# Expert rows of a two-layer encoder step in 52 blocks of 32 rows, by column groups of TensorE, with five expert buffers

## The chip, the cores and the metric

The kernel runs on one core of a Trainium2 chip. The metric is the device time of one execution in microseconds (us), the median of several. Engines are named as in the profile: PE is TensorE's matmuls, PEld its weight loads, DVE VectorE, ACT ScalarE, POOL GpSimd, SP SyncE. A name with a q (SPq, DVEq) is an engine's sequencer.

## The reference, cut to what matters

Two layers of an encoder run over 592 token rows of width 1024 in f32. Each has a mixer and then a mixture of experts. The change is in the experts (and in the layer norm after them):

```
scores = sigmoid(x @ router_w)                       # 16 experts in 4 groups of 4
grouped = scores + router_bias; best group; top 2 experts inside it
for e in range(16):
    h = silu(x @ w_gate[e]) * (x @ w_up[e])          # 1024 -> 256
    y = y + (h @ w_down[e]) * combine[..., e]        # 256 -> 1024
x = layer_norm(ALPHA * x + y)
```

Each token goes to two experts, so there are 1184 pairs of token and expert per layer, 74 per expert on average.

## The kernel before, in words

The program is written out by hand for each engine; every order is that of the code, and engines wait for each other by semaphores. The experts of a layer (`experts(l)` on each engine) work as follows.

**Slots.** Each of the 16 experts has 128 slots. VectorE ranks the tokens of each expert and writes, for each expert, five one-hot tiles of 128x128 (line 2155); TensorE multiplies them with the token numbers (line 1314), which gives the token of every slot. POOL gathers the rows of 128 slots with an indirect DMA (line 960) into one of two buffers. Where an expert has more tokens than slots, the rest goes into overflow blocks. Each engine has a loop over at most `NOV` = 9 of them (lines 768, 966, 1413, 1738, 2216), whose iterations do nothing past the count that was found.

**Work of one expert.** TensorE transposes the 128 gathered rows (line 1359, 8 transposes), ACT and DVE copy them out, then 8 matmuls of a 128x128 stationary slice of rows with 128x512 moving weights (gate and up side by side) make the hidden values in one PSUM bank (line 1371). ACT takes the exponential (line 1727), DVE forms silu and the product (lines 2182 to 2185), TensorE transposes the result (line 1379), DVE copies it, and 4 matmuls (line 1390) multiply it with the down weights, halves of 512 columns. ACT and DVE copy one half each (lines 1734, 2208), and SP stores the 128 rows to `y_rows` (line 760). Each f32 matmul call is two instructions in the trace. TensorE's order in step e is: gate and up of e, transposes of e-1's hidden values, transposes of e+1's rows, down of e-1.

**Weights.** An expert's weights are 1 MB gate, 1 MB up, 1 MB down (lines 723 to 725), all on SP's queue, in four buffers: experts e with e % 4 below 2 in `ring`, the others in `wexp` in the arena. SP loads experts 2 and 3 when attention ends, 0 and 1 when the output projection ends (`ring` holds that projection's weights until then), and expert e+4 when the down product of e is done.

**After the experts.** SP's queue also loads the next layer's weights, four items after the store of expert 13 (line 718). When the last stores have landed, POOL gathers two rows per token from `y_rows` (line 942); in layer 0 DVE adds them and norms (lines 2303 to 2330), after its loop over overflow blocks; in layer 1 TensorE adds them by diagonal matmuls (lines 1326 to 1328). The residual rows and the norm's parameters are loaded by POOL between the gathers of experts 2 and 3.

**Elsewhere.** The router's partial sums (line 1123) are matmuls with 32 stationary columns whose outputs go to PSUM partitions 0, 32, 64 and 96 in turn, so that four of them lie in four column groups of the array:

```
for k in range(KD):
    c = 32 * (k % 4)
    last = pe.matmul(ps[c:c + 32, 512 * half:512 * half + n], w[:, k, :],
                     xT[:, k, lo + n * half:lo + n * half + n], start=(k < 4), stop=(k >= 4))
```

Early in layer 0, POOL issues nine stores of zeros to the overflow rows (line 836).

## Time and profile before

| | us |
|---|---|
| median of 3 runs | 1348.32 (1345.34 to 1348.69) |
| the profiled execution's own time | 1348.82 |
| its span | 1347.0 |
| TensorE matmuls busy | 1208.0 (90%) |
| VectorE busy | 600.8 (45%) |
| ScalarE busy | 266.9 (20%) |
| lines 1371 and 1390 (gate and up, down) | 229.5 and 115.8 busy |

The span runs from the first to the last recorded instruction; the execution's own time is 1.8 us more. A line's busy time is the sum over its instructions with overlaps counted once.

### The profile page before, as it was taken

Reading aid. Unit: us, or ns where it says so; the run is one execution under the profiler, and the core shown is the slowest. Engines: PE = TensorE matmul, PEld = TensorE weight load, DVE = VectorE, ACT = ScalarE, POOL = GpSimd, SP = SyncE. Lnnn points to the kernel's source line nnn. Section 1 sums busy time; section 2 is a strip of 40 time slices with the busy share of each in tenths; the row PEclk is TensorE's granted clock in tenths of the full one; section 3 lists DMA queues with packets and bytes.
Section 4 is the critical chain, followed back from the end, with each engine's and each line's share of the span. In section 5 each row is a group of like instructions: output and inputs, shape, how many; then the busy total and the mean of one; then the engine's idle time right before and its main releaser. Section 6 shows DMA issues by size and latency. Waiting matters only on the chain.

```text
span 1347.0 us, 13706 instructions
## 1 busy us (share of the span) xinstructions
PE 1208.0 (90%) x4719; PEld 689.0 (51%) x4719; DVE 600.8 (45%) x1412; ACT 266.9 (20%) x630; POOL 223.6 (17%) x390
## 2 busy tenths in 40 slices
PE   8999999998899489999749899999999939999966
PEld 4447777544644244444325455775764424444422
DVE  2178888503624537433355120530533345744316
ACT  1204434212300001111102223322320001111110
POOL 0105444222002120000063200000001111000013
PEclk9999999999999789999969999999999959999978
DMA  8113012353461669999652410000125168999733
GB/s 335 62 63 141 1 63 79 126 187 25 60 218 57 213 195 363 362 361 369 239 188 76 167 63 0 1 0 1 63 64 187 55 230 283 356 362 370 262 141 121
DMA packets 109156, 219.23 MB, mean 163 GB/s; under 512 B 5145, under 2 KB 72281, under 8 KB 107937
## 3 DMA queue, kind: packets, MB, share of 16 engines
q1 hardware_dynamic: 90544, 153.35, 32.3%
q0 software_dynamic: 18256, 64.20, 15.2%
q8 instruction: 39, 0.64, 0.2%
q10 hardware_dynamic: 288, 0.80, 0.2%
q14 instruction: 29, 0.23, 0.1%
HBM read 183.44 MB, written 34.86 MB: 162 GB/s over the span
## 4 chain that ended last, share of the span: by engine, by line
PE 82%; DVE 8%; issue 4%; DMA 2%; ACT 2%; POOL 1%; DVEq 0%; POOLq 0%; ACTq 0%; SPq 0%
PE pair L1371 16%; PE pair L1280 10%; PE pair L1029 10%; PE pair L1390 8%; PE pair L1040 5%; PE pair L1146 5%; PE pair L1212 5%; PE pair L1464 3%; PE pair L1249 3%; PE pair L1516 2%; PE pair L1359 2%; PE pair L1070 2%; PE pair L1247 1%; PE pair L1496 1%; PE pair L1230 1%
## 5 line engine op out<-in xcount | busy, mean ns | idle before, releaser
L1029 PE MATMUL pair<-ring,xT 128*128 128x512 f32 (+1 forms) x320 | 138.9, 593 | 0.0
L1371 PE MATMUL pair<-ring,arena 128*128 128x512 f32 x256 | 117.0, 611 | 3.5 <-DVE arena L2173 3.5
L1371 PE MATMUL pair<-arena 128*128 128x512 f32 x256 | 112.5, 592 | 0.0
L1029 PEld LDWEIGHTS pair<-ring,xT 128*128 128x128 f32 (+1 forms) x320 | 57.7, 182 | 75.6 <-issue 75.1
L1146 PE MATMUL pair<-xT,ring 128*128 128x296 f32 x320 | 85.1, 421 | 6.1 <-ACT arena L1552 3.0
L807 POOL TENSOR_SCALAR small<-small 128x1 f32<-128x1 f32 (+3 forms) x45 | 15.7, 349 | 419.8 <-DVE small L2054 376.6
L1371 PEld LDWEIGHTS pair<-ring,arena 128*128 128x128 f32 x256 | 49.9, 196 | 66.6 <-issue 66.6
L2193 DVE COPY arena<-pair 128x256 f32<-128x256 f32 x32 | 13.6, 424 | 156.3 <-PE pair L1379 156.3
L829 POOL TENSOR_TENSOR arena<-arena 128x128 f32<-128x128 f32 x140 | 56.6, 438 | 158.0 <-PE pair L1072 87.9
L1371 PEld LDWEIGHTS pair<-arena 128*128 128x128 f32 x256 | 48.6, 190 | 61.2 <-issue 61.2
L1212 PE MATMUL pair<-arena 128*128 128x264 f32 (+5 forms) x280 | 76.6, 403 | 2.6 <-issue 1.4
L960 POOL DMA_INDIRECT arena<-x_rows,ints x32 | 31.0, 970 | 287.5 <-PE pair L1359 236.6
L1986 DVE TENSOR_REDUCE small<-pair 128x1 f32<-128x144 f32 (+4 forms) x40 | 22.4, 560 | 120.3 <-PE pair L1217 120.2
L1146 PEld LDWEIGHTS pair<-xT,ring 128*128 128x128 f32 x320 | 60.4, 193 | 25.6 <-issue 9.0
L1280 PE MATMUL pair<-ring,mixT 128*128 128x512 f32 (+1 forms) x160 | 72.1, 593 | 1.0 <-issue 1.0
L1280 PE MATMUL pair<-ring,xT 128*128 128x512 f32 (+1 forms) x160 | 71.9, 592 | 0.0
L1390 PE MATMUL pair<-arena 128*128 128x512 f32 x128 | 58.2, 597 | 5.2 <-DVE arena L2193 5.2
L1040 PE MATMUL pair<-arena,ring 128*128 128x296 f32 (+1 forms) x224 | 62.1, 438 | 0.0
L1464 PE MATMUL pair<-ring,xT 128*128 128x512 f32 (+3 forms) x160 | 58.8, 523 | 1.1 <-ACT xT L1543 1.1
L1390 PE MATMUL pair<-ring,arena 128*128 128x512 f32 x128 | 57.6, 592 | 0.0
L2183 DVE RECIPROCAL arena<-arena 128x256 f32<-128x256 f32 x32 | 56.1, 1753 | 1.1
L2046 DVE SCALAR_TENSOR_TENSOR rb<-xr,pair 128x1024 f32<-128x1024 f32 (+1 forms) x10 | 12.2, 1221 | 95.7 <-PE pair L1280 95.7
(347 smaller groups left out, 1859.3 us busy)
## 6 DMA issues: line engine op xcount, KB each, us to landing
arena<-in_moe_w_gate SPq DMA_DIRECT2D x16, 1024.0 KB, 6.8
arena<-in_moe_w_up SPq DMA_DIRECT2D x16, 1024.0 KB, 9.4
arena<-in_moe_w_down SPq DMA_DIRECT2D x16, 1024.0 KB, 11.3
ring<-in_moe_w_gate SPq DMA_DIRECT2D x16, 1024.0 KB, 7.3
ring<-in_moe_w_up SPq DMA_DIRECT2D x16, 1024.0 KB, 9.9
ring<-in_moe_w_down SPq DMA_DIRECT2D x16, 1024.0 KB, 11.6
y_rows<-arena SPq DMA_DIRECT2D x32, 512.0 KB, 9.7
ring<-in_even_w_in SPq DMA_DIRECT2D x5, 2048.0 KB, 7.3
```

What stands on the lines that cost most here:

```text
L829: last = pool.tensor_tensor(dst, both, mid, ALU.subtract)
L960: pool.indirect_dma_start(xg[:, e % 2, :], None, x_rows[2 * l], bass.IndirectOffsetOnAxis(ap=sloti[:, e:e + 1], axis=0)).then_inc(xg_in[e ...
L1029: last = pe.matmul(ps[0:P, 0:n], xT[:, k, 128 * i:128 * i + P], w[:, k, :], start=(k == 0), stop=(k == chunks - 1))
L1040: last = pe.matmul(ps[0:w.shape[2], 512 * s:512 * s + n], w[:, k, :], src[:, k, n * s:n * s + n], start=(k == 0), stop=(k == chunks - 1))
L1146: last = pe.matmul(ps[0:w.shape[2], 512 * s:512 * s + n], w[:, k, :], xT[:, k, n * s:n * s + n], start=(k == 0), stop=(k == KD - 1))
L1212: last = pe.matmul(ps[0:P, lo:lo + cols], q_, k_, start=(c == 0), stop=(mask is None and c == len(lq) - 1))
L1249: last = pe.matmul(out, vb[j], pT[:, n % 2, 128 * j:128 * j + P], start=False, stop=(j == nb - 1))
L1280: last = pe.matmul(ps[0:P, 512 * half:512 * half + 512], mixed(k, i), w[:, k, :], start=(k == 0), stop=(k == KD - 1))
L1371: last = pe.matmul(bank, xgT[:, e % 2, k, :], gu[:, k, :], start=(k == 0), stop=(k == KD - 1))
L1390: last = pe.matmul(psum[2][:, 512 * half:512 * half + 512], hT[:, e % 2, 128 * k:128 * k + 128], dn[:, k, 512 * half:512 * half + 512], st ...
L1464: last = pe.matmul(ps[0:P, lo:lo + n], xT[:, k, 128 * i:128 * i + P], w[:, k, :], start=(k == 0), stop=(k == KD - 1))
L2183: chain(dve.reciprocal(eg[:, b, :], eg[:, b, :]))
```

## The change

**Slots.** Experts have 96, 96, 128 and 96 slots in turn (`CAPS`), 1664 in all: 52 blocks of 32 in 13 tiles of 128 (`NX`). A tile's four blocks belong to one expert or to two neighbouring ones: tile 0 is three blocks of expert 0 and one of expert 1, tile 1 two of expert 1 and two of expert 2, and so on (`BLOCKS`); tile 8 is all expert 10, and the last, tile 12, one block of expert 14 and three of 15. All per-expert steps (gather, transposes, copies, store) are now per tile. `NOV` is 12.

**Matmuls.** In gate and up and in down, each matmul is replaced by four, one for each block: 32 stationary columns, the weights of the block's expert as the moving operand, the block's 32 PSUM partitions as output.

**Weights.** Gate and up lie side by side in DRAM, and both tensors are stored there as they lie in SBUF, so that a partition's 4096 (gate and up) or 2048 (down) words are one contiguous run. There are five buffers: two in `wexp`, two in `ring`, the fifth in `xT` (gate and up) and `mixT` (down). Experts 0 and 1 are loaded at attention's end, 2, 3 and the down weights of 4 after the output projection, the rest of 4 after the router's partial sums. For experts 5 to 15, SP issues gate and up when gate and up of the last tile of the buffer's earlier expert are in PSUM; ACT issues the down weights on its own queue, after its wait for that tile's down product and ahead of its copy of it.

**Around.** The residual rows and the norm's parameters are loaded after the last gather; tile 4's residual goes into a buffer that comes free later, and is loaded after tile 0's combine. The four items of the next layer's weights are issued after the stores of tile 10 (the first) and tile 11 (the other three). The slot numbers take two more small VectorE steps. The one-hot tiles are one instruction per expert in a tile, and the first group is tile 0 alone, then two tiles each.

```diff
-NOV = 9
-NSLOTS = (NE + NOV) * 128
+CAPS = [96, 96, 128, 96] * 4
+BASE = [sum(CAPS[:e]) for e in range(NE)]
+NX = sum(CAPS) // 128
+NOV = 12
+NSLOTS = (NX + NOV) * 128
+BLOCKS = [[next(e for e in range(NE) if BASE[e] <= 128 * x + 32 * j < BASE[e] + CAPS[e]) for j in range(4)]
+          for x in range(NX)]
+LAST = [max(x for x in range(NX) if e in BLOCKS[x]) for e in range(NE)]
+NB = 5
+PLACE = [e % NB for e in range(NE - 1)] + [1]
+BEFORE = [max((p for p in range(e) if PLACE[p] == PLACE[e]), default=None) for e in range(NE)]
...
+    parts["base"] = np.broadcast_to(np.array(BASE, np.float32), (128, 16))
+    parts["caps"] = np.broadcast_to(np.array(CAPS, np.float32), (128, 16))
 
     s3 = s[:, :, None]
...
+        x_far = [arena[:, lo:lo + D] for lo in (0, 3552)]
+        assert 3552 + D <= yg_at
         qng = r4.take(QL + KVL)
 
         def residual(s, i):
 
-            return x_far[i - 2] if s % 2 == 1 and i >= 2 else xr[:, i % 2, :]
+            return x_far[i - 2] if s % 2 == 1 and i in (2, 3) else xr[:, i % 2, :]
 
 
...
+        IX_GROUPS = [range(max(x, 0), x + 2) for x in range(-1, NX, 2)]
         LAST_IX = len(IX_GROUPS) - 1
...
-            gu = base[:, 0:2 * SLOT].rearrange("p (k n) -> p k n", k=KD)
-            dn = base[:, 2 * SLOT:3 * SLOT].rearrange("p (k n) -> p k n", k=2)
-            return gu, dn
-
-        gate_d = a["moe_w_gate"].rearrange("l e (k p) n -> (l e) p k n", p=128)
-        up_d = a["moe_w_up"].rearrange("l e (k p) n -> (l e) p k n", p=128)
-        down_d = a["moe_w_down"].rearrange("l e (k p) n -> (l e) p k n", p=128)
+            b = PLACE[e]
+            if b < 4:
+                base = (wexp if b < 2 else ring)[:, (b % 2) * 3 * SLOT:(b % 2) * 3 * SLOT + 3 * SLOT]
+                gu, dn = base[:, 0:2 * SLOT], base[:, 2 * SLOT:3 * SLOT]
+            else:
+                gu = xT[:, :, :].rearrange("p k t -> p (k t)")[:, 0:2 * SLOT]
+                dn = mixT[:, :, :].rearrange("p k t -> p (k t)")[:, 0:SLOT]
+            return gu.rearrange("p (k n) -> p k n", k=KD), dn.rearrange("p (k n) -> p k n", k=2)
+
+        gu_d, down_d = a["moe_w_gate_up"], a["moe_w_down"]
 
         def mixed(k, i):
 
...
+            def load_gate_up(l, e):
+                sp.dma_start(expert_place(e)[0], gu_d[l * NE + e]).then_inc(we_in[PLACE[e]].sem, 16)
+
+            def load_down(l, e):
+                sp.dma_start(expert_place(e)[1], down_d[l * NE + e]).then_inc(we_in[PLACE[e]].sem, 16)
+
             def load_expert(l, e):
-                gu, dn = expert_place(e)
-                s = we_in[e % 4].sem
-                sp.dma_start(gu[:, :, 0:DE], gate_d[l * NE + e]).then_inc(s, 16)
-                sp.dma_start(gu[:, :, DE:2 * DE], up_d[l * NE + e]).then_inc(s, 16)
-                sp.dma_start(dn, down_d[l * NE + e]).then_inc(s, 16)
+                load_gate_up(l, e)
...
+                sp.wait_ge(*pe_full[("wo", l, 4)])
                 load_expert(l, 2)
                 load_expert(l, 3)
-                sp.wait_ge(*pe_full[("wo", l, 4)])
-                load_expert(l, 0)
-                load_expert(l, 1)
-                for e in range(NE):
-                    if e + 4 < NE:
-                        sp.wait_ge(*dn_ps[(l, e)])
-                        load_expert(l, e + 4)
-                    sp.wait_ge(*y_sa[(l, e)])
-                    sp.wait_ge(*y_sd[(l, e)])
-                    sp.dma_start(y_rows[l][128 * e:128 * e + 128, :], yb[:, e % 2, :]).then_inc(y_st[e % 2].sem, 16)
-                    if l == 0 and e == 13:
-                        for n in range(n_items0, n_items0 + 4):
-                            load_item(n)
+                load_down(l, 4)
+                sp.wait_ge(*pe_full[("lp", l, 1)])
+                load_gate_up(l, 4)
+                for x in range(NX + 1):
+                    if x < NX:
+                        sp.wait_ge(*gu_ps[(l, x)])
+                        for e in FREED[x]:
+                            load_gate_up(l, e)
+                    if x >= 1:
+                        d = x - 1
+                        sp.wait_ge(*dn_ps[(l, d)])
+                        sp.wait_ge(*y_sa[(l, d)])
+                        sp.wait_ge(*y_sd[(l, d)])
+                        sp.dma_start(y_rows[l][128 * d:128 * d + 128, :], yb[:, d % 2, :]).then_inc(y_st[d % 2].sem, 16)
+                        if l == 0 and d == LAST[12]:
+                            load_item(n_items0)
+                        if l == 0 and d == LAST[13]:
+                            for n in range(n_items0 + 1, n_items0 + 4):
+                                load_item(n)
 
                 mk = ov[l]
                 sp.wait_ge(*ix_sb[(l, LAST_IX)])
                 count = sp.value_load(ovi[0:1, 0:1], min_val=0, max_val=NOV)
                 with sp.Fori(0, NOV) as b:
                     with sp.If(count > b):
...
+                if s % 2 == 1 and i == 4:
+                    pool.wait_ge(*(pe_full[("cb", 1, 0)] if s == 3 else cb_sb[(0, "first")]))
+                elif s % 2 == 1 and i >= 2:
+                    pool.wait_ge(*dn_ps[(s // 2, LAST[10])])
                 elif i >= 2:
                     pool.wait_ge(*r_mv[(s, i - 2)])
...
 
             def gather_rows(l, i):
...
-                        load_ln_params(2 * l + 1)
-                        for i in range(NT):
-                            load_residual(2 * l + 1, i)
                     pool.indirect_dma_start(
                         xg[:, e % 2, :], None, x_rows[2 * l],
                         bass.IndirectOffsetOnAxis(ap=sloti[:, e:e + 1], axis=0)).then_inc(xg_in[e % 2].sem, 16)
+                load_ln_params(2 * l + 1)
+                for i in range(4):
+                    load_residual(2 * l + 1, i)
                 m = ov[l]
-                pool.wait_ge(*xgT_ps[(l, NE - 1)])
+                pool.wait_ge(*xgT_ps[(l, NX - 1)])
                 count = pool.value_load(ovi[0:1, 0:1], min_val=0, max_val=NOV)
                 with pool.Fori(0, NOV) as b:
                     with pool.If(count > b):
...
             pool.dma_start(qng[:, 0:QL], a["mla_q_norm_g"][0].partition_broadcast(128)).then_inc(mg_in.sem, 16)
             pool.dma_start(qng[:, QL:QL + KVL], a["mla_kv_norm_g"][0].partition_broadcast(128)).then_inc(mg_in.sem, 16)
             layer_norm_row(1, 0)
+            load_residual(1, 4)
             scale_row(1, 1)
             for i in range(NT):
                 if i + 1 < NT:
...
             def gate_up(l, e):
-                pe.wait_ge(*we_in[e % 4][(l, e)])
+                for x in sorted(set(BLOCKS[e])):
+                    pe.wait_ge(*we_in[PLACE[x]][(l, x)])
                 pe.wait_ge(*xgT_sa[(l, e)])
                 pe.wait_ge(*xgT_sd[(l, e)])
                 if e >= 2:
                     pe.wait_ge(*h_sb[(l, e - 2)])
-                gu, _ = expert_place(e)
                 bank = psum[1][:, 512 * (e % 2):512 * (e % 2) + 512]
                 for k in range(KD):
-                    last = pe.matmul(bank, xgT[:, e % 2, k, :], gu[:, k, :], start=(k == 0), stop=(k == KD - 1))
+                    for j, x in enumerate(BLOCKS[e]):
+                        c = slice(32 * j, 32 * j + 32)
+                        last = pe.matmul(bank[c, :], xgT[:, e % 2, k, c], expert_place(x)[0][:, k, :],
+                                         start=(k == 0), stop=(k == KD - 1))
                 last.then_inc(gu_ps.sem, 1)
 
             def hidden_t(l, e):
...
-                        last = pe.matmul(psum[2][:, 512 * half:512 * half + 512], hT[:, e % 2, 128 * k:128 * k + 128],
-                                         dn[:, k, 512 * half:512 * half + 512], start=(k == 0), stop=(k == 1))
+                        for j, x in enumerate(BLOCKS[e]):
+                            c = 32 * j
+                            last = pe.matmul(psum[2][c:c + 32, 512 * half:512 * half + 512],
+                                             hT[:, e % 2, 128 * k + c:128 * k + c + 32],
+                                             expert_place(x)[1][:, k, 512 * half:512 * half + 512],
+                                             start=(k == 0), stop=(k == 1))
                 last.then_inc(dn_ps.sem, 1)
 
             def experts(l):
                 rows_t(l, 0)
-                for e in range(NE + 1):
-                    if e < NE:
...
                     if e >= 1:
                         act.wait_ge(*dn_ps[(l, e - 1)])
+                        for n in FREED[e - 1]:
+                            act.dma_start(expert_place(n)[1], down_d[l * NE + n]).then_inc(we_in[PLACE[n]].sem, 16)
...
                     chain(ts(wts, wts, 1.0 / ALPHA, None, ALU.mult))
-                chain(ts(ovn, cnt, 128.0, None, ALU.is_gt))
-                for m in (256.0, 384.0, 512.0):
+                chain(tt(cnt, cnt, const("caps"), ALU.subtract))
+                chain(ts(ovn, cnt, 0.0, None, ALU.is_gt))
+                for m in (128.0, 256.0, 384.0):
...
 
-                for e in IX_GROUPS[g]:
-                    for i in range(NT):
-                        last = ts(oneh[:, e % 2, i, :], iotab[:, :], 1.0, rk1[:, i, e:e + 1], ALU.add, ALU.is_equal)
+                for x in IX_GROUPS[g]:
+                    for e in sorted(set(BLOCKS[x])):
+                        lo, n = 32 * BLOCKS[x].index(e), 32 * BLOCKS[x].count(e)
+                        r = 128 * x + lo - BASE[e]
+                        last = tt(oneh[:, x % 2, :, lo:lo + n], iotab[:, r:r + n].unsqueeze(1).to_broadcast([128, NT, n]),
+                                  rk1[:, :, e:e + 1].to_broadcast([128, NT, n]), ALU.is_equal)
                     last.then_inc(oh_sb.sem, 1)
 
...
               "cache_fox_logf": np.asarray(inputs["cache_fox_logf"])[0, 0].T}
+    tiles_of = lambda w: np.asarray(w).reshape(2 * NE, -1, 128, w.shape[3]).transpose(0, 2, 1, 3)
+    inputs = {**inputs, "moe_w_down": tiles_of(inputs["moe_w_down"]),
+              "moe_w_gate_up": tiles_of(np.concatenate([inputs["moe_w_gate"], inputs["moe_w_up"]], 3))}
```

Three places at which the order of instructions changes follow. On TensorE, in layer 0's experts, one step in full, before (line 1390 is down, 1371 gate and up, 1379 and 1359 the transposes):

```order
L1314 MATMUL pair<-cstb,arena 128x2 x10
L1379 MATMUL pair<-cst,arena 128x128 x2
L1359 MATMUL pair<-cst,arena 128x128 x8
L1390 MATMUL pair<-ring,arena 128x512 x4
L1371 MATMUL pair<-arena 128x512 x8
```

and with the change (1409 and 1386 are the transposes, 1421 is down, 1400 gate and up):

```order
L1341 MATMUL pair<-cstb,arena 128x2 x10
L1409 MATMUL pair<-cst,arena 128x128 x2
L1386 MATMUL pair<-cst,arena 128x128 x8
L1421 MATMUL pair<-arena 32x512 x16
L1400 MATMUL pair<-ring,arena 32x512 x32
```

The transposes are the same; 4 matmuls of 128 stationary columns became 16 of 32, and 8 became 32.

On ScalarE, from one exponential to the next (and the copies after it), before (1718 copies transposed rows, 1734 the down product, 1727 is the exponential):

```order
L1727 ACTIVATE arena<-pair 128x256
L1718 COPY arena<-pair 128x512
L1734 COPY arena<-pair 128x512
L1727 ACTIVATE arena<-pair 128x256
L1718 COPY arena<-pair 128x512
L1734 COPY arena<-pair 128x512
```

and with the change, at the step that frees two experts' buffers (1751, 1769 and 1760 are the same three):

```order
L1760 ACTIVATE arena<-pair 128x256
L1751 COPY arena<-pair 128x512
L1766 DMA ring<-in_moe_w_down 128x2048
L1766 DMA mixT<-in_moe_w_down 128x2048
L1769 COPY arena<-pair 128x512
L1760 ACTIVATE arena<-pair 128x256
```

Two loads of down weights stand ahead of the copy of the down product.

On SyncE, at the end of layer 0's experts, before (718 are the next layer's weights, 760 the stores of expert rows, 767 the read of the overflow count):

```order
L723 DMA arena<-in_moe_w_gate 128x8x256
L724 DMA arena<-in_moe_w_up 128x8x256
L725 DMA arena<-in_moe_w_down 128x2x1024
L760 DMA y_rows<-arena 128x1024 x3
L718 DMA ring<-in_mla_w_in 128x8x512
L718 DMA ring<-in_mla_w_in 128x8x320
L718 DMA ring<-in_mla_w_uk 128x2x1024
L718 DMA ring<-in_mla_w_uv 128x2x1024
L760 DMA y_rows<-arena 128x1024 x2
```

and with the change (731, 783 and 792 are the same):

```order
L783 DMA y_rows<-arena 128x1024 x2
L734 DMA arena<-in_moe_w_gate_up 128x4096
L783 DMA y_rows<-arena 128x1024 x3
L731 DMA ring<-in_mla_w_in 128x8x512
L783 DMA y_rows<-arena 128x1024
L731 DMA ring<-in_mla_w_in 128x8x320
L731 DMA ring<-in_mla_w_uk 128x2x1024
L731 DMA ring<-in_mla_w_uv 128x2x1024
L783 DMA y_rows<-arena 128x1024
```

Three of the four items now stand between the last two stores, where before all four stood ahead of the last two.

## Rows read from the trace of the kernel before

**Rows 1.** Page, part 2: TensorE's busy tenths and clock in 40 slices.
```profile
PE   8999999998899489999749899999999939999966
...
PEclk9999999999999789999969999999999959999978
```

**Rows 2.** Windows: us, busy by engine, clock, DMA share, GB/s; start, then expert stage.
```profile
5.00:15.00 10.00, 9.45 (x28) 6.89 (x29) 0.00 (x0) 0.00 (x0) 0.00 (x0) 1.00 1.04 432
600.00:640.00 40.00, 40.00 (x125) 19.95 (x124) 17.16 (x27) 5.64 (x11) 2.87 (x3) 1.00 1.05 371
```

**Rows 3.** Timeline of TensorE late in layer 0's experts: start, duration, line.
```profile
639.95 7.03 PE L1371 MATMUL pair<-arena 128*128 128x512 f32 x16
...
647.90 3.60 PE L1390 MATMUL pair<-ring,arena 128*128 128x512 f32 x8
651.34 7.03 PE L1371 MATMUL pair<-arena 128*128 128x512 f32 x16
```

**Rows 4.** Timelines of the column-grouped line 1123, and its weight loads (ns min/median/max).
```profile
1076.59 1.92 PE L1123 MATMUL pair<-xT,vecs 128*32 128x512 f32 x16 [1.10 <-ACT xT L1543]
...
235.47 2.20 PE L1123 MATMUL pair<-xT,vecs 128*32 128x296 f32 x32
...
L1123 PEld LDWEIGHTS pair<-xT,vecs x96: 106/110/177, 235.5 to 1082.6; 128*32 128x32 f32 x96
```

**Rows 5.** Chain of waits: start, duration, what; last steps ahead of layer 0's experts.
```profile
466.72 1.73 DVE arena L2155 x10
...
469.45 0.83 issue
470.28 4.26 DMA arena<-x_rows,ints
...
477.49 9.22 PE pair L1371 x16
```

**Rows 6.** Timeline of VectorE: one product over 128x256.
```profile
490.39 0.42 DVE L2184 TENSOR_TENSOR arena<-pair,arena 128x256 f32<-128x256 f32 x1
```

**Rows 7.** Line 725: time on SyncE's queue (ns min/median/max), then landing.
```profile
L725 SPq DMA_DIRECT2D ring<-in_moe_w_down x16: 1531/2718/4786, 447.8 to 1234.8; - x16
...
DMA to landing us min/median/max: 9.8/11.4/14.3
```

**Rows 8.** Timeline of ScalarE: copy of an expert's output, next exponential.
```profile
500.42 0.59 ACT L1734 COPY arena<-pair 128x512 f32<-128x512 f32 x1 [2.85 <-PE pair L1390]
507.28 0.39 ACT L1727 ACTIVATE arena<-pair 128x256 f32<-128x256 f32 x1 [6.28 <-PE pair L1371]
```

**Rows 9.** Timeline of SyncE's queue at the end of layer 0's experts.
```profile
652.81 1.44 SPq L718 DMA_DIRECT2D ring<-in_mla_w_in  x2
...
663.61 5.17 SPq L760 DMA_DIRECT2D y_rows<-arena  x2
```

**Rows 10.** Chain of waits from layer 0's last store to its combine.
```profile
668.42 5.31 DMA y_rows<-arena
...
675.98 0.06 DVEq L2217
...
676.69 0.06 DVEq L2217
...
681.30 1.29 DVE arena L2303
```

**Rows 11.** Layer 1: chain, loop on TensorE (ns, first and last start), timeline.
```profile
1296.25 2.73 DMA y_rows<-arena
...
L1413 PEldq COMPARE_BRANCH  x18: 86/220/229, 669.9 to 1303.7; - x18
...
1306.64 2.04 PE L1326 MATMUL pair<-xr,arena 128*128 128x512 f32 x2 [11.20 <-DMA arena<-y_rows,ints]
```

**Rows 12.** Timeline of POOL: the nine stores of zeros and the work after them.
```profile
118.19 4.99 POOL L836 DMA_DIRECT2D y_rows<-xr  x9
124.10 2.59 POOL L829 TENSOR_TENSOR arena<-arena 128x128 f32<-128x128 f32 x7 [0.92 <-ACT arena L1567]
```

110 lines of the change are left out of this document (54 added, 56 removed).

## The prediction

> **What bounds the kernel now.** I read the page first, for the engine that is busy: TensorE's matmuls are busy nine tenths or more in most slices of the span, and the granted clock is nearly full in most of them [rows 1]. Then windows of the expert stage: in 40 us of it TensorE is busy all 40 at full clock, and the DMA engines have no gap either, moving 371 GB/s [rows 2]. Two resources are full at once, so the timeline has to say who waits. In it gate and up of one expert starts at 639.95 and that of the next at 651.34, 11.39 us later, with nothing idle between: 7.03 for gate and up, 3.60 for down (their tails overlap what follows), the transposes in the rest [rows 3]. So TensorE sets the pace and DMA only just keeps up. What is worth something here is a whole step of 11.39 us, as long as the weights come in time.
>
> **Term 1, three steps fewer per layer.** 16 steps become 13. A step keeps its transposes, copies, exponential and store; what must be priced is the new matmul form, since a step now issues 96 instructions on 32 columns (64 for gate and up, 32 for down) where it issued 24 on 128. The kernel has this form already: line 1123 puts four matmuls of 32 stationary columns and different moving data into four column groups. Its 16 instructions over 512 moving columns take 1.92 us, its 32 over 296 take 2.20 [rows 4]. At full width, 16 instructions over 512 take 7.03 [rows 3]. 8 take 3.60 [rows 3], so an instruction is (7.03 - 3.60) / 8 = 0.43 and the tail of the last one 0.17; without that tail the grouped form takes 1.75 / 4 = 0.44 per four. Four groups run in the time of one, with their weight loads inside. So 64 instructions are 16 such fours, 6.9 us as before, and the step stays at 11.39. Six steps go: 6 x 11.39 = **-68.3 us**. Nothing else covers this time, since TensorE is idle nowhere in the step.
>
> **Term 2, the head.** The first gather now waits for the one-hots of tile 0 alone. Before, the chain has ten instructions, 1.73 us, then 0.83 until POOL starts, 4.26 for the rows [rows 5]. Now there are two, over 480 and 160 elements per partition; a product over 256 takes 0.42 [rows 6], so at most 1.05. Gain 0.7 a layer: **-1.4**. Against it: expert 4's gate and up are the last of 9.4 MB (experts 2 and 3, the rest of 4) queued from 447 on. At 432 GB/s, which loads of long runs reach early in the kernel [rows 2], they end at 469; at 371 at 472.5, and then the gather shares the engines for up to 3 us. I count nothing and keep 3 us for the range, since the new layout has the long runs.
>
> **Term 3, the loop over overflow blocks.** `NOV` goes from 9 to 12, on five engines. On DVE in layer 0 the loop starts when the last store lands and ends just as the gathered rows come, at 681.30; one empty iteration is 676.69 - 675.98 = 0.71 us [rows 10]. Three more are **+2.1** in full. In layer 1 TensorE's loop ends at 1303.9, and the combine starts at 1306.64, released by the gather [rows 11]; 2.1 more ends it at 1306.0, just hidden. ACT's and POOL's loops end earlier still.
>
> **Term 4, the last store of layer 0.** It is queued behind loads on SP's queue. Now, with four items issued from 652.81 on, ahead of the last two stores [rows 9], it takes 5.31 to land [rows 10], in layer 1 without them 2.73 [rows 11]. With the change three of them, 3.4 MB, stand between the last two stores. From the first of these stores to the landing of the last is 10.2 us now (4.8 between the two issues, of which the second lasts some 0.4 of the 5.17 [rows 9], then 5.31). Then 3.4 MB and two stores of 0.52 MB must pass: 4.5 MB at 432 to 371 GB/s is 10.4 to 12.1, and the landing about 1.4 behind the last byte, so 11.8 to 13.5. I take the middle: **+2.5**.
>
> **What I cost at nothing.** ACT's loads: one of 1 MB is on SP's queue for 1.5 to 4.8 us there [rows 7], behind two others; on ACT it stands ahead of the copy of the down product, and ACT has 6.28 us free behind that copy [rows 8]. One fits. Where two stand together (tiles 3 and 7) the worst is 9.6 us, and the copy would be up to 2.2 too late for the next down product (11.39 - 3.43 = 8.0 us after the last): 9 us in all for four places, kept below. Queued behind the ACT load are that copy, the next exponential, and with it DVE's silu, which has a whole gate and up of slack. Residual rows and norm parameters come some 20 us ahead of the combine; tile 4's residual is issued by POOL after tile 0's store and has three tiles of work ahead of it. Two more VectorE steps on slot numbers lie in a step in which VectorE is mostly idle. POOL's three further stores of zeros are about 1.7 us; its next work waited 0.92 for ACT anyway [rows 12], so at most 0.8 shows.
>
> **The weights' supply.** Expert 15 is needed when tile 12 starts, 12 x 11.39 = 137 us after tile 0. From the end of tile 0's gate and up (7 us), 11 x 3.15 MB of weights, 23 transfers of 0.52 MB, and up to 5.2 MB of residuals, parameters and the first item must pass: 46.7 to 51.9 MB. At 432 GB/s that ends at 115 to 127, at 371 at 133 to 147. The new layout makes 371 the bound that holds least. Ends: no stall, or 10 us a layer. I take no stall, since 432 is what loads of such runs reached.
>
> **Sum.** -68.3 - 1.4 + 2.1 + 2.5 = -65.1. The span 1347.0 becomes 1281.9, the execution 1283.7 (it is 1.8 longer). The profiled execution, 1348.8, lies 0.5 above the median of the runs, so **1283** for the median, with 1276 to 1291 for this case by the bounds above.
>
> **Rivals.** (B) *Late weights.* Loads of down weights are issued when the product is done, and for experts 6, 7, 8, 12, 13 and 15 the tile that needs them starts 11.4 us later. Line 725's land 9.8 to 14.3 after issue, median 11.4 [rows 7]. For it: these are just too long. Against: there 2 MB stand ahead on the same queue, here none. At 14.3, 2.9 late at twelve places is 35 us; with the 9 of ACT the worst is 1327; half of the lateness, 22, gives 1305.
> (F) *Supply stays at 371 GB/s* and all of the 51.9 MB stand ahead: 10 us late per layer, 1303. For it: only the first microseconds show more. Against: there the runs were long, as they are now. The Trainium skill (DMA: Bandwidth & Descriptors, Specifications) gives about 358 GB/s as a core's limit at the HBM; by an estimate from it the last weights come up to 15 us late per layer, and the sum is 1313. The 432 of this trace [rows 2] does not agree with that as a limit for this core alone.
> (C) *The four groups overlap less.* If in each four one weight load of 0.11 us [rows 4] does not hide, a four takes 0.54; 24 fours a step, 26 steps, +0.11 each: +69, so 1352. Against it: the 0.44 of line 1123, weight loads included. The Trainium skill (TensorE: Matmul & The Clock Gate, Measured speedup vs the span model) says three column tiles of 32 over 512 gained 2.38 times, not 3; by an estimate from that a four takes 0.54 too.
> (D) *Slower.* The weight loads and streams of the groups go one after the other, as they may when the moving data come from four places of SBUF. With all four loads outside, 0.44 more per four, 24 x 26 x 0.44 = 275: 1558. It decides from 0.53 per four on (65 us over 624 fours is 0.10). Line 1123 speaks against this too, its moving data also lie in four places.
> (E) *It does not do what it says:* an expert has more tokens than slots, and an overflow block runs. Counting the router's choices on the reference's inputs, I get at most 92 for an expert of 96 slots and 97 for one of 128. One block would be in series: rows 4.3, weights 11.4, matmuls 10, hidden values and stores 7, about 33 us: 1316.
>
> **Chances.** Forecast 0.76; B 0.11; F 0.04; C 0.04; D 0.03; E 0.02. The range 1276 to 1304 takes in the forecast with its bounds, F, and the lower half of B. A difference under 0.3% (4 us) cannot be told from none. Faster: forecast, B, F, E, 0.93. C straddles the line: 0.03 same, 0.01 slower, and with D slower is 0.04.
>
> **What would show it.** Right: gate and up starts 11.4 us apart in 13 steps, 7.0 us for its 64 instructions; TensorE idle nowhere in them; the first gather 0.7 earlier; DVE's loop 2.1 longer and on the chain; the last store of layer 0 landing near 7.8 us after issue. Wrong: a wait of TensorE on the loads of `in_moe_w_down` or `in_moe_w_gate_up`, most of all in tiles 4 to 6, 9, 10 and 12, with a clock of 0.5 behind it (B, F); steps over 13 us with no idle time (C, D); line 1454 or the gathers of overflow blocks in the trace (E).

## The result and the profile after

The changed kernel takes **1308.04 us** (median of 4, 1306.13 to 1308.65), the kernel before beside it 1348.51: a ratio of 0.9701, 95% interval 0.9682 to 0.9720. That is 40 us faster, where 65 were forecast, and above the range of 1276 to 1304. The profiled execution took 1306.13, with a span of 1303.9 us.

The page, part 2, TensorE and its clock beside [rows 1]: still a full engine, with much the same dips.
```profile
PE   8999999999899759999549899999999957999965
...
PEclk9999999999999969999869999999999978999978
```

Cut at five places, the span of 1347.0 became 1303.9 like this (the forecast by its own terms in the last column):

| stretch | before | after | change | forecast |
|---|---|---|---|---|
| start to first gate/up, layer 0 | 477.5 | 475.3 | -2.2 | -0.7 |
| layer 0: to the end of the last down | 190.1 | 163.8 | -26.3 | -34.2 |
| to the first gate/up of layer 1 | 437.9 | 444.7 | +6.8 | +3.9 |
| layer 1: to the end of the last down | 189.9 | 165.7 | -24.2 | -34.2 |
| to the end | 51.6 | 54.4 | +2.8 | 0 |

Only the expert stages gain, and each 8 to 10 us less than three steps of 11.39. The chain of waits says why. First an undisturbed step, late in layer 0:
```profile
599.56 6.87 PE pair L1400 x64
606.43 0.37 PE pair L1409 x2
...
607.67 3.57 PE pair L1421 x32
611.24 0.84 PE pair L1400 x5
```
(1400 is gate and up, 1409 and 1386 the transposes, 1421 down.) Nothing is idle, and gate/up of one tile starts 11.68 us before the next (611.24 - 599.56), not 11.39. The timeline of the same step, which can be set beside [rows 3], has 8.22 from the start of gate/up to the start of down (599.38 to 607.60), where [rows 3] has 7.95, and 3.46 from down to the next gate/up, against 3.44. So the work itself costs what [rows 4] promised, and 0.27 us lie between gate/up and down, where full-width transposes stand between column-grouped matmuls.

At the head of layer 0 the one-hots are shorter, but the gather behind them is longer than the 4.26 of [rows 5]:
```profile
463.82 0.91 DVE arena L2194 x2
...
466.61 5.72 DMA arena<-x_rows,ints
```
In the 5.7 us of the gather, SyncE's queue still moves 0.95 MB of weights; in the 4.3 us before it moved none.

The second piece, the chain at tile 3 of layer 0:
```profile
499.30 0.18 DVE ints L2206
499.48 0.26 issue
499.74 9.02 DMA arena<-x_rows,ints
508.80 1.09 PE pair L1386 x8
```
Its rows are asked for when VectorE has written their slot tokens, at 499.5, land 9.0 us later, and TensorE has waited 2.4 us. In layer 1 it is 2.5.

The third, tile 9, the chain in layer 0 and in layer 1:
```profile
582.28 3.57 PE pair L1421 x32
585.86 1.82 issue
587.68 7.07 PE pair L1400 x64
...
1193.85 2.56 issue
1196.42 8.77 PE pair L1400 x64
```
This "issue" ends when the weights of expert 12 are there, the last block of tile 9. ScalarE issued its down weights at 574.24, and they took 13.3 us. The row of `in_moe_w_down` between 573 and 583 us says so; the second fence has the two transfers of gate and up, for experts 13 and 14, that SyncE's queue had issued before them:
```profile
L1766 ACTq DMA_DIRECT2D ring<-in_moe_w_down x1: 334/334/334, 574.2 to 574.2; - x1
...
DMA to landing us min/median/max: 13.3/13.3/13.3
```
```profile
569.42 0.33 SPq L734 DMA_DIRECT2D ring<-in_moe_w_gate_up  x1
569.79 0.55 SPq L734 DMA_DIRECT2D xT<-in_moe_w_gate_up  x1
```
These down weights are not what tile 9's gate and up work on. One semaphore counts both loads of an expert, and `gate_up` waits for its full count (line 1391). Expert 12's gate and up weights were issued at 557.74 and landed 12.0 us later; tile 9's down product, the first to use the down weights, starts at 607.60, 20 us after they landed. So the code's wait is what lets this load hold up TensorE. No run here has the wait split in two.

Windows (columns as in [rows 2]) show the DMA engines full around that, at 366 to 421 GB/s in five of 5 us from 565 to 590 us, 401 on average, and after layer 1's longer wait a granted clock of 0.80, which is what makes gate/up 8.77:
```profile
570.00:575.00 5.00, 5.00 (x50) 1.82 (x52) 4.38 (x7) 0.97 (x2) 0.94 (x1) 1.00 1.06 421
...
1196.40:1205.00 8.60, 8.58 (x64) 2.83 (x64) 0.00 (x0) 0.00 (x0) 0.00 (x0) 0.80 0.82 318
```

The fourth is the chain behind layer 0's last down, beside [rows 10]. The store takes 11.69 us to land, not 5.31, with three loads issued between the last two stores (SyncE's queue, second fence).
```profile
639.17 0.70 DVE arena L2248
639.94 11.69 DMA y_rows<-arena
...
652.45 0.99 POOL arena L969
...
653.74 5.30 DMA arena<-y_rows,ints
...
659.16 1.30 DVE arena L2343
```
```profile
635.51 0.33 SPq L783 DMA_DIRECT2D y_rows<-arena  x1
636.01 0.39 SPq L731 DMA_DIRECT2D ring<-in_mla_w_in  x1
636.51 0.90 SPq L731 DMA_DIRECT2D ring<-in_mla_w_uk  x1
637.52 0.59 SPq L731 DMA_DIRECT2D ring<-in_mla_w_uv  x1
639.94 0.36 SPq L783 DMA_DIRECT2D y_rows<-arena  x1
```
From the issue of the store before it (635.51) to the landing, 4.49 MB pass at a mean of 279 GB/s.

The fifth is POOL's closing drain, after its last store was issued; before and after:
```profile
L149 POOLq DRAIN  x1: 6782/6782/6782, 1340.0 to 1340.0; - x1
```
```profile
L160 POOLq DRAIN  x1: 9885/9885/9885, 1293.8 to 1293.8; - x1
```

### The profile page after: what moved, and what is told of

It is laid out like the page before. It is cut to its first block, busy times and chain, and to the rows that moved or that the text cites. A ratio compares the mean times of both kernels' runs of the same rounds, so it can differ in the third digit from the quotient of the medians.

```text
span 1303.9 us, 16801 instructions
## 1 busy us (share of the span) xinstructions
PE 1145.3 (88%) x6357; PEld 614.1 (47%) x6357; DVE 567.9 (44%) x1258; ACT 257.3 (20%) x612; POOL 220.7 (17%) x387
## 4 chain that ended last, share of the span: by engine, by line
PE 78%; DVE 9%; DMA 5%; issue 4%; ACT 2%; POOL 1%; SPq 0%; POOLq 0%; DVEq 0%; ACTq 0%
PE pair L1400 12%; PE pair L1307 11%; PE pair L1056 11%; PE pair L1421 6%; PE pair L1067 5%; PE pair L1173 5%; PE pair L1239 5%; PE pair L1497 3%; PE pair L1276 3%; PE pair L1549 2%; DMA arena<-x_rows,ints 2%; PE pair L1386 2%; PE pair L1097 2%; PE pair L1529 2%; PE pair L1274 2%
## 5 line engine op out<-in xcount | busy, mean ns | idle before, releaser
L1400 PE MATMUL pair<-ring,arena 128*32 128x512 f32 x608 | 128.5, 595 | 0.0
L1400 PE MATMUL pair<-arena 128*32 128x512 f32 x736 | 105.1, 628 | 7.9 <-issue 4.4
L983 POOL DMA_INDIRECT arena<-x_rows,ints x26 | 26.4, 1014 | 267.3 <-PE pair L1386 162.4
L1421 PE MATMUL pair<-ring,arena 128*32 128x512 f32 x304 | 65.3, 595 | 3.8 <-DVE arena L2233 3.8
L1400 PEld LDWEIGHTS pair<-arena 128*32 128x32 f32 x736 | 30.7, 115 | 67.9 <-issue 67.9
L1400 PEld LDWEIGHTS pair<-ring,arena 128*32 128x32 f32 x608 | 33.8, 110 | 57.4 <-issue 57.3
L1400 PE MATMUL pair<-xT,arena 128*32 128x512 f32 x320 | 56.3, 592 | 0.0
L1576 ACT COPY xT<-pair 128x1024 f32<-128x1024 f32 (+1 forms) x15 | 14.2, 948 | 209.2 <-PE pair L1048 209.2
```

The costliest lines, as they stand in the source:

```text
L983: pool.indirect_dma_start(xg[:, e % 2, :], None, x_rows[2 * l], bass.IndirectOffsetOnAxis(ap=sloti[:, e:e + 1], axis=0)).then_inc(xg_in[e ...
L1400: last = pe.matmul(bank[c, :], xgT[:, e % 2, k, c], expert_place(x)[0][:, k, :], start=(k == 0), stop=(k == KD - 1))
L1421: last = pe.matmul(psum[2][c:c + 32, 512 * half:512 * half + 512], hT[:, e % 2, 128 * k + c:128 * k + c + 32], expert_place(x)[1][:, k, 51 ...
```

## The experiments

My theory after the result: four separate causes (the step's boundaries, tile 3's slot tokens, tile 9's weights, the last store), each with its own cure, and a fifth, the drain, without one. Spans and stages below are of the profiled executions. The start of layer 0's experts scatters between 473 and 481 us among them, and one execution of each kernel was profiled, so small effects are read from the stages, not from the time.

### 1. The column groups alone, on the kernel before

```diff
-    last = pe.matmul(bank, xgT[:, e % 2, k, :], gu[:, k, :], start=(k == 0), stop=(k == KD - 1))
+    for j in range(4):
+        c = slice(32 * j, 32 * j + 32)
+        last = pe.matmul(bank[c, :], xgT[:, e % 2, k, c], gu[:, k, :],
+                         start=(k == 0), stop=(k == KD - 1))
```
and the same for down.

> The kernel before, with nothing changed but its gate/up and down matmuls: each full-width one becomes four that take 32 columns of slots each, all four against the same expert's weights, so no block or buffer differs. **Theory (the step of 11.68 us after, against 11.39 before, is paid where the column-grouped matmuls meet full-width ones):** the step becomes about 11.7 us here too, +0.29 x 32 steps, so some +9 us, near 1357.8 us. **Rival (the 0.29 us comes from the change's other parts, its different weights side by side or its later vectors):** the step stays 11.39 us and the time 1348.5. **Third case (the four groups overlap less when they read the same weights than when they don't):** the gate/up piece, 7.03 us before, grows well past 7.1.

Measured: 1357.12 us, ratio 1.0053 (1.0033 to 1.0072). Its chain:
```profile
583.64 6.87 PE pair L1373 x64
590.50 0.37 PE pair L1382 x2
...
591.75 3.57 PE pair L1395 x32
595.32 1.70 PE pair L1373 x13
```
Piece by piece this is the step of the changed kernel, 11.68 us, with no new block, buffer or queue. The theory holds: the form costs 0.29 us a step, and the different weights side by side cost nothing.

### 2. Column groups in down only

> The kernel before with only its down matmuls in four groups of 32 columns (gate/up full width), to see where between the pieces the 0.29 us of a step are paid. **Theory (each boundary between column-grouped and full-width matmuls costs, on the way in and on the way out):** two boundaries a step are left of four, the row transposes to down and down to gate/up, and the step is about 11.39 + 0.13 = 11.52 us by the shifts seen in the changed kernel (row transposes to down +0.10, down to gate/up +0.03). **Rival (the cost is one of the down piece itself, 3.64 us against 3.60, or of the weight loads):** 11.43 us or less, or all 0.29 us, 11.68.

Measured: 1356.75 us in a single run, so only its steps are read. The chain of the kernel before, then this one's:
```profile
640.11 6.87 PE pair L1371 x16
646.97 0.22 PE pair L1379 x2
...
648.07 3.44 PE pair L1390 x8
```
```profile
585.57 7.07 PE pair L1371 x16
592.63 0.22 PE pair L1379 x2
...
593.72 3.57 PE pair L1392 x32
597.29 1.91 PE pair L1371 x4
```
The step is 11.72 us, longer than with all matmuls grouped; both theory (11.52) and rival missed. I had counted four boundaries in a step of the changed kernel. There are two: gate/up to the transposes, and the transposes to down; down to the next gate/up stays in column groups. This kernel has two as well, transposes to down and down to gate/up, and pays 0.34 for them against 0.29. The chains show each by itself: grouped gate/up to transposes makes their piece 0.37 in place of 0.22 (experiment 1), transposes to grouped down makes down 3.57 in place of 3.44 (both), and grouped down to full-width gate/up makes that 7.07 in place of 6.87 (here). So a boundary between a column-grouped and a full-width matmul costs 0.13 to 0.20 us, about 0.15, and grouped to grouped nothing. The Trainium skill (TensorEngine Tiling (Array Packing), Key Properties) says that a change of tiling mode drains TensorE, without a price; these rows agree.

### 3. Slot tokens in pairs from tile 0

```diff
-        IX_GROUPS = [range(max(x, 0), x + 2) for x in range(-1, NX, 2)]
+        IX_GROUPS = [range(x, min(x + 2, NX)) for x in range(0, NX, 2)]
```

> The changed kernel, with the slot tokens formed for tiles 0 and 1 together, then 2 and 3, and so on, as the kernel before does, in place of tile 0 alone and then 1 and 2, 3 and 4. **Theory (tile 3's row gather is late because its slot tokens are formed one step later than before):** TensorE's wait at tile 3's row transposes, 2.38 us in layer 0 and 2.54 us in layer 1, goes; the head pays for one more pair, about 0.7 us in each layer as it did before; in sum -3.5 us, 1304.5. **Rival (the gather is late for its own DMA's sake, since weights of the first experts are read beside it):** the wait stays within 0.5 us and the head's cost comes on top, 1309.5.

Measured: 1304.28 us (1294.72 to 1305.97), ratio 0.9656 (0.9630 to 0.9682). The chain at tile 3 of layer 0 has no wait left:
```profile
500.07 6.87 PE pair L1400 x64
...
508.42 3.57 PE pair L1421 x32
```
The step there goes from 14.53 to 11.92 us, in layer 1 from 14.69 to 11.93. The span fell by 2.7, since tile 9's wait in layer 0 grew to 2.0 us and this time the clock fell behind it too (gate/up 8.77). The cause is shown: the regrouping meant for the head took a step from tile 3.

### 4. Expert 14's gate and up one tile later

```diff
+FREED_GU = [list(f) for f in FREED]
+FREED_GU[7].remove(14)
+FREED_GU[8].append(14)
...
-                        for e in FREED[x]:
+                        for e in FREED_GU[x]:
```

> The changed kernel, with expert 14's gate and up weights (2.1 MB) issued after tile 8 instead of after tile 7. **Theory (expert 12's down weights, and with them tile 9, are late because they share the DMA engines with the 4.2 MB of gate and up of experts 13 and 14 issued just before them):** the down weights land some 8 us after issue instead of 13.4, tile 9's wait of 1.83 us (layer 0) and 2.57 us (layer 1) goes, and with it the gate/up of 8.77 us at a lowered clock in layer 1 becomes 7.05; about -6 us, 1302. **Rival (ScalarE issues these down weights too late, after its copy's wait, whatever else is on the DMA engines):** the wait stays within 0.5 us in both layers and the time 1308. **Second rival:** a stall of the same size appears where expert 14 is needed, at tiles 10 or 11, for it has a step less; 1308 too, with the wait elsewhere.

Measured: 1300.99 us, ratio 0.9651 (0.9631 to 0.9671). The chain from tile 8's down to tile 9 has no wait:
```profile
580.07 3.57 PE pair L1424 x32
583.64 6.87 PE pair L1403 x64
```
Nor has it in layer 1, where gate/up is 7.05 again; expert 12's down weights land 8.9 us after issue, not 13.3. Nothing waits for expert 14. The stages are 160.5 and 161.4 us, 3.3 and 4.3 shorter. Theory confirmed; ScalarE's place in it is not the cause. The wait of gate and up for both loads stays as it was; this edit only makes the down weights land ahead of it.

### 5. The attention weights around the last stores

```diff
                         if l == 0 and d == LAST[12]:
-                            load_item(n_items0)
-                        if l == 0 and d == LAST[13]:
-                            for n in range(n_items0 + 1, n_items0 + 4):
+                            for n in range(n_items0, n_items0 + 3):
                                 load_item(n)
+                        if l == 0 and d == NX - 1:
+                            load_item(n_items0 + 3)
```

> The changed kernel, with the attention weights that it loads near the end of layer 0's experts moved: the three items that followed tile 11's or 12's store now go out after tile 10's, the last one after the last store. **Theory (the last store of layer 0 lands 11.7 us after its issue, against 4.6 to 6 for others, because items of 36 KB to 2 MB are read beside it):** the store lands some 4 to 5 us after its issue, the row gathers behind it start 6 to 7 us sooner; but the DVE loop over the overflow tiles, which ends at 659.09 us where the gathers land at 659.04, then bounds the combine, so that only 0 to 2 us of it come through; 1306 to 1308. **Rival (no loop bound, the loop's end follows the store's):** all of it comes through, -7 us, 1301. **Second rival (the store is slow by itself, as the last one with nothing but its rows):** no change.

Measured: 1301.88 us, ratio 0.9651 (0.9636 to 0.9666).
```profile
640.66 3.92 DMA y_rows<-arena
...
645.40 0.99 POOL arena L969
...
646.69 5.61 DMA arena<-y_rows,ints
...
652.40 1.29 DVE arena L2343
```
The store lands in 3.9 us and the rows are there at 652.3: the stretch between the layers is 437.6 us, 7.1 less. All of it came through, so the rival was right. My theory had the loop's end as a fixed time; it starts when the last store has landed, and moved with it.

### 6. Nine overflow tiles

`NOV = 9` in place of 12.

> The changed kernel with 9 overflow tiles in place of 12, so three zero stores on POOL less and three empty loop iterations less on every engine. **Theory (an empty iteration costs DVE 0.53 us, but DVE's loop only ties with the row gathers, which take 7.5 us from the last store's landing):** layer 0's combine starts at most 0.2 us earlier, and the time is 1308 +-1. **Rival (the prediction's own: the loop bounds the combine):** 3 x 0.53 = -1.6 us in layer 0. **Second question:** after the last output store POOL's closing drain takes 9.9 us in the changed kernel and 6.8 us in the kernel before, with the store itself landed some 3 us after issue in both. If the number of overflow tiles (their loop or their zero stores) sets it, the drain is 6.8 us here and the time another 3 us shorter; if not, 9.9 us.

Measured: 1306.43 us, ratio 0.9681 (0.9656 to 0.9706), profiled 1305.1 us of span. The loop ends 1.6 us ahead of the combine here, which still starts 7.5 us after the store's landing, with the gathers. The loop does not bound it, and the drain is 9.885 us again, so the number of overflow tiles doesn't set that either.

### 7. Down weights on SyncE's queue

```diff
-                        for n in FREED[e - 1]:
-                            act.dma_start(expert_place(n)[1], down_d[l * NE + n]).then_inc(we_in[PLACE[n]].sem, 16)
...
                         sp.wait_ge(*dn_ps[(l, d)])
+                        for n in FREED[d]:
+                            load_down(l, n)
                         sp.wait_ge(*y_sa[(l, d)])
```

> The changed kernel, with the down weights of experts 5 to 15 issued on SyncE's queue, after the same down matmuls as now, in place of ScalarE's. **Theory (the DMA engines are full around tile 9, so that the two queues only share them):** expert 12's down weights stand behind 4.2 MB of gate and up on one queue and land within 2 us of the 587.7 us they land at now; ScalarE loses 11 issues of 0.33 us a layer that nothing waited for; 1308 +-2. **Rival A (a second queue is what lets down weights pass the gate and up loads):** waits appear at the down matmuls of other tiles too, 5 to 15 us slower. **Rival B (issuing behind the copy's wait on ScalarE costs something):** 2 us or more faster.

Measured: 1306.65 us, ratio 0.9697 (0.9673 to 0.9720). Tile 9 waits 1.93 and 2.54 us, as before, and no other tile waits for weights. Which queue issues the down weights makes no difference here, for good or ill.

### 8. to 10. The size of the pieces

Three kernels leave the weights, or some of them, in the reference's order of rows (the views go back to `.rearrange("l e (k p) n -> (l e) p k n", p=128)` for these). First all of them:

> The changed kernel, with the expert weights in the reference's order of rows, so that each partition reads gate and up in 8 pieces of 2 KB and down in 2 of 4 KB, in place of one piece of 16 KB and one of 8 KB. **Theory (between 565 and 595 us the DMA engines are busy all the time at 366 to 421 GB/s, so bytes per second set when tile 9's weights land; 2 KB pieces run slower, as in the kernel before at 371 GB/s):** the stall at tile 9 grows from 1.8 to 2.6 us to some 4 to 6 us in each layer and others appear behind it, +5 to +10 us, 1313 to 1318. **Rival (the size of the pieces makes no difference at 2 KB):** 1308.

Measured: 1302.96 us (1299.70 to 1310.23), ratio 0.9651 (0.9632 to 0.9670). The theory fell, and not by chance: tile 9 did not wait in either layer, with the DMA engines full at 390 to 405 GB/s. The profiled execution is the slowest of the four, 1310.23: its steps at tile 3 take 17.5 and 16.2 us. So what counted at tile 9 was who got the bytes. Two kernels to tell whose pieces:

> The changed kernel, with gate and up read in pieces of 2 KB and down still in pieces of 8 KB; with both short (2 and 4 KB), tile 9's wait was gone in both layers though the DMA engines moved no more bytes per second. **Theory (the two queues take turns piece by piece, so that a queue's share goes by the size of its pieces: down has 8 of 24 parts in the changed kernel and has 8 of 10 here):** expert 12's down weights land within 9 us of their issue, tile 9 doesn't wait in either layer, and the gates and ups land later, which nothing waits for; 1302. **Rival (down's own shorter pieces made it, or chance):** tile 9's wait of 1.8 to 2.6 us is there, 1308.

> The changed kernel, with gate and up in pieces of 16 KB and down in pieces of 4 KB. **Theory (queues share by the size of their pieces; down has 4 of 20 parts here):** expert 12's down weights still land with the last of the bytes issued before them, so tile 9's wait stays and grows by 0 to 1 us a layer; 1308 to 1310. **Rival (shorter down pieces are what removed the wait):** no wait at tile 9, 1302.

Measured: short gate and up, 1306.94 us, ratio 0.9676 (0.9654 to 0.9698), tile 9 without a wait in both layers, down weights landed after 7.6 us; short down, 1317.35 us, ratio 0.9759 (0.9737 to 0.9781), tile 9 waits 2.9 and 5.1 us, more than the theory's growth of 0 to 1, tile 6 now 2.0 in both layers, expert 12's down weights landing after 14.4. The queues' rows show the turns, in stretches in which both queues have work (columns: queue, packets, MB, share of 16 engines; q1 is SyncE's, q10 ScalarE's, a packet is a piece). The changed kernel from 579 to 583 us, then short gate and up from 578.2 to 580.2, then short down from 584 to 588:
```profile
q1 hardware_dynamic: 63, 1.03, 63.4%
q10 hardware_dynamic: 58, 0.48, 28.2%
```
```profile
q10 hardware_dynamic: 83, 0.68, 82.2%
q1 hardware_dynamic: 83, 0.16, 20.6%
```
```profile
q1 hardware_dynamic: 68, 1.11, 70.5%
q10 hardware_dynamic: 68, 0.28, 17.5%
```
The theory is shown with its rule of turns: as many pieces of one queue as of the other (nearly so in the first), whatever their size, so that down gets a third of the two queues' bytes at 16 and 8 KB, four fifths at 2 and 8 KB, a fifth at 16 and 4 KB. POOL's queue takes its turn too: 62 pieces of up to 4 KB in the first stretch. In the first 3 us after the issue none of ScalarE's pieces has passed yet, in any of the three; the rest of the landing time is the share. The Trainium skill (DMA: Bandwidth & Descriptors, Queues, rings and completion order) says that each DMA engine takes turns between queues, a packet of several descriptors at a time. The equal counts agree with turns; that the changed kernel's down pieces pass evenly, 13 to 16 in each microsecond from 578 to 583, speaks for turns of a single piece here, but no run settles that. The time of short gate and up didn't fall as forecast, because in layer 1 tile 3's wait for its rows, 2.3 us, was followed by a granted clock of 0.50, and the step took 17.4 us (14.7 in the changed kernel, where a wait of 2.5 us left the clock at 1.00).

### 11. Three edits together

Experiments 3, 4 and 5 in one kernel.

> The changed kernel with three edits at once: slot tokens in pairs from tile 0 (alone: profiled span 1301.2 us against 1303.9), expert 14's gate and up one tile later (alone: 1297.8) and the attention weights around the last stores (alone: 1298.4). **Theory (three separate causes, each on TensorE's or the stores' own stretch of the path):** the gains add, -2.7 -6.1 -5.5 us, and without the lowered clock that tile 9 brought when its wait grew to 2.0 us, near 1289.6 us of span and 1292 us. **Rival (they share a cause: earlier experts only meet later weights, so what one edit gives the next wait takes):** no more than the best edit alone, 1298 to 1301.

Measured: **1288.06 us** (1284.76 to 1291.57), ratio 0.9556 (0.9537 to 0.9575), span 1282.5. The stages are 157.9 and 158.1 us (13.6 less in all), the stretch between the layers 438.6 (6.1 less). Past the head no tile waits for rows or weights any more, and the gains add: the causes are separate. They even more than add: the three medians alone lie 3.8, 7.1 and 6.2 us under the changed kernel's, 17.0 in sum, and together it is 20.0, 4 us below the 1292 expected. Most of the rest is the cost that experiment 3 alone had at tile 9, 2.2 us more than the changed kernel in the profiled executions, which is gone here. The stages stay 2.0 and 2.3 us above the forecast's 155.9 and 155.8. Thirteen tiles' boundaries are 3.5 us; against them stand shorter first steps (10.3 and 10.8 us, 11.0 in the kernel before) and one group of slot tokens fewer.

### 12. The last residual on SyncE's queue

Added to 11; the rows of token tile 4 in layer 1 are loaded as follows (the semaphore and TensorE's wait for it are left out here):

```diff
+            sp.wait_ge(*pe_full[("cb", 1, 0)])
+            sp.wait_ge(*x_st[0][(2, 4)])
+            sp.dma_start(residual(3, 4)[0:TILES[4]], x_rows[2][512:512 + TILES[4], :]).then_inc(last_in.sem, 16)
```

> The kernel with the three edits (1288.06 us; profiled 1282.5 us of span), with one more: the residual rows of the last token tile in layer 1, which POOL loads amid the last stores in the changed kernel and long before in the kernel before, are loaded from SyncE's queue. **Theory (this late load by POOL is why POOL's closing drain takes 9.885 us in the changed kernel and in each variant of it, and 6.782 us in the kernel before):** the drain takes 6.8 us and the time is 3 us less, 1285. **Rival (the drain depends on something else that the change brings, such as how many row gathers POOL has issued):** the drain stays 9.885 us and the time 1288 +-1. A side effect of up to 0.6 us in each direction is possible, since POOL issues one transfer less and the residual comes by another queue.

Measured: 1290.75 us, ratio 0.9578 (0.9559 to 0.9599); the drain 9.803 us. Theory fallen. The drain was 6.782 us in the kernel before and both its variants, 9.885 in the changed kernel and all its variants but this one. What of the change lengthens it stays open.

## Why the prediction was right or wrong

The span fell by 43.1 where 65.1 were forecast, 22.0 short, by its own steps:

- **Term 1, three steps fewer**, right in kind: gate/up takes what it did and TensorE is idle in no plain step. The sentence that failed is "the step stays at 11.39". It is 11.68, since [rows 4] price column groups among themselves and not their meeting with full-width transposes. 13 tiles, two layers, 0.27 each: 7.0 us (experiments 1 and 2).
- **Term 2, the head.** The one-hots did shorten, by 0.8 us a layer, but nothing of it arrived. The gather behind them took 5.7 us in both layers, not 4.3 and 4.2, since expert 4's weights were still passing: the "up to 3 us" that the text counted at nothing came to 1.5. From the one-hots to the first gate/up it is 11.5 and 11.4 us, against 10.8 and 10.7 before, and 11.4 and 11.1 in experiment 3, which has the old pairs. And the text stopped at the head: the same regrouping forms tile 3's slot tokens a step later. It cost 2.6 and 2.8 us, 5.4 in all (experiment 3).
- **The weights' supply, "I take no stall".** The total was right: 401 GB/s passed on average around tile 9 with all engines full, so rival F's 371 did not hold there. But the sum over all bytes says nothing of their order. Expert 12's down weights took turns with 4.2 MB that were issued before them and needed later: 2.0 us in layer 0 and 4.5 in layer 1 with the clock's part, 6.5 in all (experiment 4). They held up gate and up only because its wait counts both loads; the prediction priced a late down load as late for the tile and did not ask when its product comes. This is rival B's mechanism at one of the six experts it named, at 6.5 us instead of 22; its transfer lengths (9.8 to 14.3 us, [rows 7]) were the right ones, its "here none", for what stands ahead, was not, since another queue's bytes do.
- **Term 4, the last store**, right in kind, too small: from down's end to the landing it is 12.5 us, against 6.1 before, +6.4 and not +2.5 (experiment 5). I had 11.8 to 13.5 us from the store before it to the landing; it was 16.1, since the 4.5 MB, rightly counted, passed at a mean of 279 GB/s and not at 371 to 432. The 1.4 us behind the last byte stand in no row; in the kernel before, 0.02 MB pass in the last store's last 1.2 us and none in its last 0.4.
- **Term 3, the loop**, wrong: 12 empty iterations take 6.4 us, as 9 did before. One takes 0.53 us and not 0.71. It ends at 659.1, level with the gathers, so 2.1 us were not spent, and three iterations fewer bring nothing (experiment 6).
- **At nothing:** ScalarE's loads, rightly (0.33 us of its queue for most; experiment 7). The end of the kernel, wrongly: +2.8, of which the longer drain is 3.1; not explained.
- **Rivals C, D and E** didn't come: at the full clock a four takes 0.44 us (7.05 / 16), and no overflow block ran.

Together 7.0 + 5.4 + 6.5 + 3.9 - 2.1 + 2.8 = 23.5. The start of layer 0's experts, 1.5 earlier than forecast, lies within its scatter, which hides the head's loss there. That leaves 22.0. Smaller differences, -1.1 in the stages and +1.1 between them, cancel; layer 1's head, 1.4 worse than forecast, is in the latter. The range failed because the chance of 0.76 stood on "no stall", "same step" and a short store at once, each of which had a price in the text, while the range was taken from rivals in which only one of them fails.

## What to carry to other kernels

Price a new matmul form together with its neighbours: count the boundaries between forms in a step, not only the instructions (0.15 us each here). When weights are reloaded under way, check each transfer against the bytes issued ahead of it on every queue, by due time, not the sum of all; reordering one load of 2 MB was worth 6 to 7 us, and a queue with longer pieces takes more of the engines. Look, too, at what each wait counts: here matmuls stood still for weights that they do not use. And where a change regroups work to start one tile sooner, follow each later tile too.

## What the runs showed that I had not expected

Two queues that both have work share the DMA engines by pieces, not by bytes: SyncE's moved 1.03 MB and ScalarE's 0.48 at pieces of 16 and 8 KB, 0.16 and 0.68 at 2 and 8 KB. The length of TensorE's wait does not tell whether the clock falls behind it: at tile 9, 1.82 us left gate/up at 7.07 us, and 2.02 and 2.56 us were followed by 8.77; but at tile 6 of the kernel with short down 2.01 us left 7.07, and at tile 3 of layer 1 a wait of 2.5 us was followed by a clock of 1.00 in the changed kernel and one of 2.3 by 0.50 in that with short gate and up. An empty iteration of a loop on VectorE took 0.53 us in one program and 0.71 in another with the same branches. POOL's closing drain took 6.8 us in one and 9.8 to 9.9 in the other, whatever was done to the loop, the queues or the last load.
